# Four of twelve ring slots per expert refilled from ScalarE's DMA queue instead of SyncE's, in a mixture-of-experts kernel

## The reference, cut to what matters

```python
top_val, top_idx = lax.top_k(logits, TOP_K)          # 4 of 32
gates = jax.nn.softmax(top_val, axis=-1)
...
gu = xb @ w_gate_up[e] + b_gate_up[e]                # 1024 x 2048 weights
gate = jnp.minimum(gu[:, :D_EXPERT], SWIGLU_LIMIT)
up = jnp.clip(gu[:, D_EXPERT:], -SWIGLU_LIMIT, SWIGLU_LIMIT)
act = (up + 1.0) * gate * jax.nn.sigmoid(SWIGLU_ALPHA * gate)
yb = act @ w_down[e] + b_down[e]                     # 1024 x 1024 weights
return yb * wt.astype(yb.dtype)[:, None]
...
out = jax.ops.segment_sum(y.reshape(n_rows, d), row_tok, num_segments=n_tok)
```

## Time and profile before

| | us |
|---|---|
| median of 3 runs | 1319.78 |
| lowest, highest | 1319.22, 1320.02 |
| span of the profiled execution | 1318.7 |
| TensorE matmuls busy in it | 1266.5 |
| VectorE busy | 516.0 |
| ScalarE busy | 191.2 |

### The profile page before, as it was taken

How to read it: one execution, slowest core, us unless ns; L and a number is a source line. 1 busy time by engine, 2 the same in 40 slices (tenths; PEclk the granted TensorE clock), 3 DMA queues, 4 the chain that set the end, 5 groups by cost and what they waited for, 6 DMA issues and landing times.

```text
span 1318.7 us, 52720 instructions
## 1 busy us (share of the span) xinstructions
PE 1266.5 (96%) x21837; PEld 745.6 (57%) x21837; DVE 516.0 (39%) x1734; ACT 191.2 (14%) x439; POOL 162.9 (12%) x267
## 2 busy tenths in 40 slices
PE   8999999999999999999999999999999999988885
PEld 4545655445565665565565665656656655645552
DVE  6554223347243343343343333333433433422237
ACT  3431123332000000000000000000000000000002
POOL 4100430122101001011011011011011010100111
PEclk9999999999999999999999999999999999999998
DMA  7453131509999999999999999999999999999997
GB/s 235 140 188 125 33 130 51 219 33 374 414 395 410 417 415 416 411 416 416 418 408 416 409 418 414 417 412 417 413 410 417 414 416 407 417 418 417 419 422 286
DMA packets 96888, 455.73 MB, mean 346 GB/s; under 512 B 11057, under 2 KB 23018, under 8 KB 63498
## 3 DMA queue, kind: packets, MB, share of 16 engines
q1 hardware_dynamic: 92784, 445.69, 83.9%
q0 software_dynamic: 3888, 8.40, 1.7%
q10 hardware_dynamic: 106, 0.04, 0.0%
HBM read 432.53 MB, written 23.27 MB: 346 GB/s over the span
## 4 chain that ended last, share of the span: by engine, by line
PE 57%; DMA 39%; DVE 2%; issue 1%; POOL 0%; SPq 0%; DVEq 0%; ACT 0%; POOLq 0%; ACTq 0%
DMA ring<-in_w_gate_up_dram 22%; PE ps L1892 20%; DMA ring<-in_w_down_dram 16%; PE ps L1468 11%; PE ps L1944 9%; PE ps L1488 4%; PE ps L1858 3%; PE ps L1529 2%; DMA x_rows_dram<-cat,rowi 1%; PE ps L1884 1%; PE ps L1522 1%; PE ps L1924 1%; PE ps L1935 1%; PE ps L1430 0%; DMA ring<-x_rows_dram 0%
## 5 line engine op out<-in xcount | busy, mean ns | idle before, releaser
L1892 PE MATMUL ps<-ring,cat 128*32 128x256 f32 x9856 | 553.6, 381 | 11.1 <-DMA ring<-in_w_gate_up_dram 10.9
L1892 PEld LDWEIGHTS ps<-ring,cat 128*32 128x32 f32 x9856 | 304.2, 110 | 229.9 <-DMA ring<-in_w_gate_up_dram 14.7
L1944 PE MATMUL ps<-ring,cat 128*32 128x256 f32 x4800 | 276.1, 379 | 13.3 <-DMA ring<-in_w_down_dram 13.1
L1944 PEld LDWEIGHTS ps<-ring,cat 128*32 128x32 f32 x4800 | 142.1, 110 | 119.1 <-DMA ring<-in_w_down_dram 19.1
L1468 PE MATMUL ps<-hbuf,ring 128*128 128x512 f32 x320 | 147.7, 607 | 1.7 <-DVE hbuf L917 1.7
L1262 DVE TENSOR_REDUCE wslot<-ps 128x2 f32<-128x6 f32 x75 | 12.3, 164 | 318.7 <-ACT cat L843 317.1
L596 POOL DMA_INDIRECT pair_rows_dram<-cat,rowi x73 | 72.8, 998 | 445.3 <-ACT cat L843 445.3
L835 ACT ACTIVATE cat<-cat 128x128 f32<-128x128 f32 x154 | 47.7, 310 | 529.6 <-DVE cat L1286 529.6
L1858 PE MATMUL ps<-hbuf,cat 128*32 128x256 bf16 x2432 | 104.9, 273 | 1.1 <-DVE cat L1386 1.1
L1286 DVE TENSOR_SCALAR cat<-ps 128x128 f32<-128x128 f32 x154 | 44.7, 291 | 135.9 <-PE ps L1892 135.8
L1468 PEld LDWEIGHTS ps<-hbuf,ring 128*128 128x128 f32 x320 | 58.8, 191 | 68.4 <-issue 66.7
(11 more groups left out here) (363 smaller groups left out, 818.7 us busy)
## 6 DMA issues: line engine op xcount, KB each, us to landing
ring<-in_w_gate_up_dram SPq DMA_DIRECT2D x256, 1024.0 KB, 10.0
ring<-in_w_down_dram SPq DMA_DIRECT2D x128, 1024.0 KB, 10.0
ring<-in_w_in_dram SPq DMA_DIRECT2D x10, 1024.0 KB, 6.3
pair_rows_dram<-cat SPq DMA_DIRECT2D x4, 2048.0 KB, 11.0
ring<-pair_rows_dram SPq DMA_DIRECT2D x4, 2048.0 KB, 20.6
ring<-in_w_out_dram SPq DMA_DIRECT2D x1, 4096.0 KB, 12.7
ring<-in_x_dram SPq DMA_DIRECT2D x4, 512.0 KB, 5.3
x_rows_dram<-ring SPq DMA_DIRECT2D x2, 1024.0 KB, 10.5
```

Of the source, the lines that this page charges most:

```text
L1892: last = mm(ps[SLOTS * q:SLOTS * (q + 1), banks[half], 0:2 * P].rearrange("p (s j i) -> p s j i", s=2, j=4), x[:, SLOTS * u:SLOTS * (u + 1 ...
L1944: last = mm(ps[SLOTS * q:SLOTS * (q + 1), 1, 0:QD], actT[:, c // 4, SLOTS * (c % 4):SLOTS * (c % 4 + 1)], w[:, i, q * QD:(q + 1) * QD], st ...
```

## The change

`refill(e)` on SP steps through units 0 to 7 only. The slots that the down units 8 to 11 of position e leave are refilled by a new function on ScalarE, `refill_down(e)`. ScalarE's single loop over all blocks becomes one loop per position, and `refill_down(e-1)` stands ahead of the loop of position e, so behind the output copy of the last block of position e-1. ScalarE reads the expert's number and the loop's bounds from `tab` by register loads. `refill_down` has no wait of its own: neither for `w_used` (the output copy has waited for it) nor for number n - 4.

```diff
-                for u in range(NU):
+                for u in range(NGU):
                     n = NU * e + u + RING
                     if n >= NU * E:
                         continue
 
                     landed = n - AHEAD
                     sp.wait_ge(w_used, used + (u + 1))
-                    if e == 0 and u >= NGU:
-                        sp.wait_ge(side_ps, 4 + 2 + u + 1 - NGU)
                     sp.wait_ge(slot_in[landed % RING], (landed // RING + 1) * 16)
                     load_unit(following[n // NU - e], n % NU, n % RING)
...
-            blocks = act.value_load(tab[0:1, E:E + 1], min_val=E, max_val=MAXB)
             with act.Fori(2, first) as g:
                 activate(g)
...
-            with act.Fori(first, blocks) as g:
-                activate(g)
+
+            def refill_down(e):
+
+                after_next = act.value_load(tab[0:1, VISIT + e + 2:VISIT + e + 3], min_val=0, max_val=E - 1)
+                for u in range(NGU, NU):
+                    n = NU * e + u + RING
+                    act.dma_start(unit_dst(n % RING, n % NU), unit_src(after_next, n % NU)).then_inc(slot_in[n % RING], 16)
+
+            upto = first
+            for e in range(1, E):
+                if e + 1 < E:
+                    refill_down(e - 1)
+                begin, upto = upto, act.value_load(tab[0:1, e + 1:e + 2], min_val=2, max_val=MAXB)
+                with act.Fori(begin, upto) as g:
+                    activate(g)
```

## The result

The changed kernel takes **1452.04 us** (median of 4 runs, 1450.55 to 1457.26) against 1319.9 us for the kernel before (4 runs): a ratio of 1.1009, 95% interval 1.0988 to 1.103. It is 132 us slower. The direction was forecast, the size was not: 1392 us was predicted, with a range up to 1442.

A forecast was written before the change was run, and what follows sets the result against it. Weights and matmuls were taken as both full and nearly level. Standstills in three-block positions (+62.8 us) and the clock (+10) made 73 us on 1319.8, about 1392 us; range 1335 to 1442 us.

The forecast's parts named there:

- the place: First block of a three-block position: down unit 11, used as soon as landed, has no slack.
- The knock-on: After each standstill TensorE frees slots 8.3 us later and the engines run dry, losing 6.7 us of transfer time.
- first term: Down-unit standstills in twelve three-block positions, 8.3 us then 5.1 each under equal queue shares: +62.8 us.
- number 47: Transfer of position 3's last down unit, issued at 398.96 and used at 409.27 us; claimed to become 8.3 us late.
- two to one against SP: Rival: engines alternate row by row, SP's down units get a third; 8.5 us per later pair, 1432 to 1442 us; chance 0.20.
- second term: TensorE's clock falling after twelve longer standstills, 1.7 us each: between 0 and 20 us, taken as +10.
- the lead of 1.6 us: Lateness of freed slots in a pair that is free, since a landing took 6.5 us where 4.9 is the least.
- SP's pacing priced at nothing: SP's wait for the number four below, now sometimes ScalarE's and landed long before: no cost.
- ScalarE's own work, hidden: Register loads and four issues per position, under 3 us, done before the next sigmoid is due: no cost.
- The last six positions at 0: Two-block positions from 1143 us on, bound by weights before and after: taken as 0, bounds 0 and 10 us.
- No change: Rival: engines serve transfers in order of issue, so down units land as before: 1319.8 us; chance 0.08.
- faster: Rival: more transfers in flight fill pauses between units: 1305 us; chance 0.03.

The follow-up runs named there:

- e2: Changed kernel with ScalarE refilling only behind the twelve three-block positions and SP doing all other refills: 1321.23 us, ratio 1.0001 to the kernel before.
- e3: Changed kernel with ScalarE refilling behind all positions except the twelve three-block ones, SP doing those: 1454.0 us, ratio 1.1005 to the kernel before.
- e5: Changed kernel with each down unit read as 128 rows of 8 KB instead of 256 of 4 KB (wrong result): 1390.81 us, ratio 1.0542.
- e8: Kernel before with down units read as 128 rows of 8 KB (wrong result): 1311.63 us, ratio 0.9929.
- e7: Changed kernel with throwaway matmuls ahead of down units 10 and 11 in each three-block position's first block: 1431.88 us, ratio 1.0853.
- e9: Changed kernel with ScalarE refilling only down unit 11's slot and SP's limit AHEAD at 5 instead of 4: 1346.04 us, ratio 1.0185.
- e13: Changed kernel with SP's limit AHEAD at 8 instead of 4: 1451.4 us, ratio 1.099 to the kernel before.
- e11: Changed kernel with ScalarE refilling only the slots of down units 10 and 11, SP the rest: 1413.97 us, ratio 1.07.
- e14: Changed kernel with ScalarE refilling only the slots of down units 10 and 11 and AHEAD at 6 instead of 4: 1390.79 us, ratio 1.0532.
- e10: Kernel before with SP's limit AHEAD at 8 instead of 4, all in one queue: 1320.69 us, ratio 0.9997.
- e12: Kernel before with down units in 8 KB rows and gate-up halves taking every second column, so the result is right: 1337.79 us, ratio 1.0122.

## Why the prediction was wrong

**Right: the direction, the bound and the place.** Weights and matmuls were level, no bandwidth lay idle, and the one exposed spot was the down units of a three-block position with ScalarE's four issued beside them. e2 and e3 show it: 1.0001 against 1.1005. The knock-on was right too: TensorE frees the next slots late and the engines run dry (572 to 581 us). SP's twelve groups of quick issues of this kind now stand (1240.36 - 435.33)/11 = 73.2 us apart, where 62.25 was the rule:

```profile
435.33 2.96 SPq L367 DMA_DIRECT2D ring<-in_w_down_dram  x4
...
1240.36 2.96 SPq L367 DMA_DIRECT2D ring<-in_w_down_dram  x4
```

**Wrong, first term: "With equal shares ... number 47 is 8.3 us late".** The step that failed is the equal division between the queues. SP's queue got 0.36 of the engines and not a half, and the standstill was about 8.5 us in each pair, not 5.1. The rival "two to one against SP" had 8.5 (and 8 to 10 us was its sign in "What would show it"), and e5 shows that the length of the rows is what makes it: take it away and the time is 1391 us. That this is the 1392 of the forecast is chance: some 9 us of it are e8's, and even with equal shares e5 stands 3.7 to 4.1 us in eleven of the twelve pairs where the forecast had 5.1, while its matmul time is 29 us up (1295.6 us busy) where the forecast had 10. The packet sizes from which that rival followed stood in the earlier trace rows; I put them behind an estimate that each engine alternates by whole sixteenths of a unit. That was my reading of "DMA: Bandwidth & Descriptors", section "Queues, rings and completion order", in the Trainium skill. That engines take turns the runs bear out: units of both queues land in turn between 626 and 639 us. That a turn is a whole sixteenth of a unit, with equal bytes for both queues, they don't (0.36 to 0.64). The standstills in the twelve positions grew by 96.4 us; the forecast had 62.8, the rival 102.

**Wrong, second term: "Each such fall costs 3.4/2 = 1.7 us".** The price came from the one fall in the tail of before, which lasts 3.4 us. Here the clock is at 0.50 for all of 629.50 to 639.70, 10.2 us, and the matmuls' busy time grows by 32.4 us where I had taken 10 and bounded it at 20. The standstills are longer (3.5 and 4.9 us, 1.9 us of work apart), and so is the fall. Taken away (e7), it gives back about 20 us, which is the bound and twice what I took. As a sum of what is seen in the trace the rival's 102 and the clock's 32 make 134, near the measured 132; the range had allowed for 122.

**Wrong in the small: the lead of 1.6 us.** I let every delay be 1.6 us cheaper. One overtaking transfer (e9) makes TensorE stand 1.5 to 2.0 us in most pairs, where the lead would leave 0.9; with equal shares (e5) it stands about 1 us less than the lead would leave; in the changed kernel the same lead did fit, 8.4 against 8.5. I can't say from these runs how much of a lead there is.

**SP's pacing priced at nothing**: right for the change (e13), but not for its reason: ScalarE's numbers had not "landed long before", SP waited for them; and wrong as a rule (e11 and e14). **ScalarE's own work, hidden**: right; its issues end 2.7 us after the copy began, and its sigmoid waits for VectorE 528.9 us in all where it waited 529.6. **The last six positions at 0**: right. From the last quick issue to the end of the span it is 1318.7 - 1110.42 = 208.3 us before and 1448.8 - 1240.36 = 208.4 after; the wait moved from the gate-up units to the down units there, as said above. **No change and faster** are out by the result itself, and the reasons given for them by e3 and e10.

## What to carry to other kernels

When weights and matmuls are level, look for the transfer with no slack before moving any other to a second queue: what is needed last must not be issued beside what is needed first, since a second queue doesn't wait its turn (e3 against e2). Then look at the rows of both: here the queue with the short rows got the smaller share, 0.36. And a limit on transfers in flight that counts numbers must be counted again when some of the numbers go elsewhere.

## What the runs showed of the hardware that was not expected

- Two queues with 8 KB and 4 KB rows shared the DMA engines 0.64 to 0.36 (a unit of the short rows every 6.86 us), with 8 KB on both one to one (every 4.86 us).
- 4 KB rows cost some time by themselves: 1 MB units of w_down in 8 KB rows made the kernel before 0.71% faster (e8, 0.9902 to 0.9955).
- TensorE's clock fell to half as a standstill of 3.5 us ended, and stayed there for 10.2 us, through 1.9 us of work, a standstill of 4.9 us and 3.2 us of work.
- With the ring read at a stride of two float32 instead of in a row, a gate-up matmul took 389 ns in the mean instead of 381 (e12).
